# The end of the first attention in a two-block forward pass: where the weights of the next products wait, and how three groups of heads are summed

## The reference

```python
h = rms_norm(h_res, norm_w)                         # 512 tokens x 1024
z = h @ w_in
for g in range(3):                                  # windows and dilations differ by group
    o_g, m_g, d_g = dilated_window_attention(q, k, v, bias, window, dilation)
wts = dens * exp(maxes - max(maxes, axis=0))        # one weight for a group, token and head
o_a = sum(wts * outs, axis=0) / sum(wts, axis=0)
y_a = (o_a * silu(g_a)) @ w_proj_a                  # g_a: 512 columns of z
# the recurrence then begins with its own columns of z
q_b, i_b, zf_fwd, zf_bwd = ...                      # 1024 columns each
lb = cumsum(softmax(lb_fwd), axis=0)                # lower bounds of the decay, one row of 1024
```

## Time and profile before

| | us |
|---|---|
| median of three executions | 4303.97 |
| the profiled execution, its own time | 4302.56 |
| its span, first to last instruction | 4300.8 |
| TensorE busy | 3535.7 |
| mean granted TensorE clock, 1 = 2.4 GHz | 0.895 |
| from the last value product (467) to the first recurrence value product (661.30) | 194 |

### The profile page before, as it was taken

One profiled execution on the slowest core, in us unless ns is written; L12 is line 12 of the kernel. 1 busy time (PEld: TensorE's weight loads), 2 busy tenths in 40 slices (PEclk: granted clock), 3 DMA queues, 4 the chain that ended last, 5 costly groups with the idle time before them and its releaser, 6 DMA issues. The chain is left out here.

```text
span 4300.8 us, 51314 instructions
## 1 busy us (share of the span) xinstructions
PE 3535.7 (82%) x21676; PEld 2057.9 (48%) x21676; DVE 1204.6 (28%) x2331; ACT 639.2 (15%) x1235; POOL 322.4 (7%) x463
## 2 busy tenths in 40 slices
PE   7998678898897877759959999698876899867766
PEld 3767437656552344437833333255766736522222
DVE  2213230232232113867230000033444334320000
ACT  1104100100111011233110000112321012100000
POOL 0000000000000000000011111103534100010000
PEclk9997889988898988879969999899776799889999
DMA  3110122243345120000269999721010201289999
GB/s 127 59 39 1 40 83 88 80 146 115 108 150 205 40 66 9 15 30 1 79 235 396 397 397 394 264 94 30 17 20 13 104 35 67 107 323 401 403 403 358
DMA packets 263928, 638.54 MB, mean 148 GB/s; under 512 B 63876, under 2 KB 114772, under 8 KB 256406
## 3 DMA queue, kind: packets, MB, share of 16 engines
q1 hardware_dynamic: 253654, 612.20, 38.3%
q0 software_dynamic: 10048, 23.07, 2.3%
HBM read 594.18 MB, written 41.05 MB: 148 GB/s over the span
## 5 line engine op out<-in xcount | busy, mean ns | idle before, releaser
L380 PE MATMUL bank<-weights_l,hT_l 128*128 128x256 f32 (+3 forms) x1552 | 485.0, 475 | 24.0 <-DMA weights_l<-in_w_in 19.6
L380 PEld LDWEIGHTS bank<-weights_l,hT_l 128*128 128x128 f32 (+1 forms) x1552 | 337.1, 221 | 169.4 <-issue 103.1
L376 PE MATMUL bank<-hT_l,weights_l 128*128 128x512 f32 (+1 forms) x928 | 332.3, 520 | 29.2 <-DMA weights_l<-in_w_in 23.8
L1739 PE MATMUL bank<-expert_weights_l,expert_tokensT_l 128*32 128x512 f32 x3072 | 339.9, 599 | 10.9 <-DMA expert_weights_l<-in_moe_w 9.4
L1944 PE MATMUL bank<-expert_weights_l,expert_tokensT_l 128*64 128x512 f32 x1024 | 238.4, 611 | 84.3 <-DMA expert_weights_l<-in_moe_w 83.1
L376 PEld LDWEIGHTS bank<-hT_l,weights_l 128*128 128x128 f32 x928 | 179.5, 194 | 179.7 <-issue 155.5
L1242 PE MATMUL bank<-hT_l,gate_weights_r 128*128 128x512 f32 x384 | 211.7, 703 | 21.1 <-DMA gate_weights_r<-in_w_in 21.1
L1739 PEld LDWEIGHTS bank<-expert_weights_l,expert_tokensT_l 128*32 128x32 f32 x3072 | 107.2, 111 | 229.1 <-issue 222.2
L1613 POOL DMA_INDIRECT expert_rows_l<-normed_rows,row_numbers_l x16 | 15.4, 961 | 2630.0 <-DMA row_numbers_l<-selected_rows 2625.7
L1944 PEld LDWEIGHTS bank<-expert_weights_l,expert_tokensT_l 128*64 128x64 f32 x1024 | 78.5, 139 | 233.6 <-issue 175.9
L1774 PE MATMUL bank<-expert_weights_l,rows 128*32 128x512 f32 x1536 | 167.8, 592 | 0.9 <-ACT rows L1814 0.9
(11 more groups left out here) (495 smaller groups left out, 4777.2 us busy)
## 6 DMA issues: line engine op xcount, KB each, us to landing
expert_weights_l<-in_moe_w SPq DMA_DIRECT2D x192, 2048.0 KB, 25.1
ada_weights_r<-in_ada_w SPq DMA_DIRECT2D x48, 1024.0 KB, 5.0
weights_l<-in_w_in SPq DMA_DIRECT2D x10, 2048.0 KB, 7.7
weights_l<-in_w_in SPq DMA_DIRECT2D x16, 1024.0 KB, 5.3
gate_weights_r<-in_w_in SPq DMA_DIRECT2D x12, 1024.0 KB, 6.1
weights_l<-in_od_w_in SPq DMA_DIRECT2D x7, 1024.0 KB, 5.4
gate<-gate_rows_r SPq DMA_DIRECT2D x24, 256.0 KB, 2.4
weights_l<-in_ev_w_in SPq DMA_DIRECT2D x3, 2048.0 KB, 10.5
```

The costliest lines, as they stand in the source:

```text
L376: ins = pe.matmul(bank[:n, :m], w_sb[:, k, s:s + n], xT[:, k, t:t + m], start=k == 0, stop=k == kt - 1)
L380: ins = pe.matmul(bank[:rows_of_tile(x), :n], x, w_sb[:, k, :n], start=k == 0, stop=k == kt - 1)
L1739: return pe.matmul(bank[q * STRIP:(q + 1) * STRIP, :], xs[:, k, e, g * STRIP:(g + 1) * STRIP], w[:, j, h * HALF:(h + 1) * HALF], start=k = ...
```

## The change

- In `first_attention` the gate's weights are loaded into the idle buffer `ya` as soon as SyncE has issued the last weight load of the value products. `merge_groups` gets that view as `ya` and a semaphore.
- `merge_groups` loads `ones` right behind `pair_rows`. After the turned rows it prefetches both chunks of `w_proj_a` and calls `ahead()`, which loads 256 columns of query weights into two idle tiles of `X`.
- The vector chain of the group weights is issued ahead of the gate products, and the gate products run beside it.
- The twelve products follow the gate. Their emptying now does the sums pair by pair: group 0 writes `oT` directly, group 1 is multiplied and added, group 2 is multiplied, added and multiplied by the gate.
- The store of `ya` isn't waited for before the recurrence; `gated_recurrence` takes the 256 query columns as a third ring slot, and prefetches the next two chunks. VectorE waits for the store only after the value products.

```diff
-        self.slot_free = [0, 0]
+        self.slot_free = [0, 0, 0]
...
+            gate_w = ya[:, :, :].rearrange("p t (a n) -> p (t a) n", n=AW)
             with core.weight_ring(512):
                 early = prefetch(core, KT, I["w_in"], 0, AW)
                 first_norm(core, I, C, X, x_landed, ya, hT)
+                normed = core.filled.n
...
+            nc.sync.wait_ge(core.filled.sem, normed)
+            weight_load(gate_w, I["w_in"], KT, OFF_GA, AW)(nc.sync).then_inc(gate_landed.sem, gate_landed.sixteen())
...
     core.load(pair[:, :, :], I["pair_rows"])
+    core.load(C["ones"][:, :, :], I["ones"].rearrange("d s t -> s d t"))
...
     with core.weight_ring(512):
-        dense(core, hT, KT, SEQ, I["w_in"], OFF_GA, AW,
-              lambda e, ct, t0, n, ps: e.activation(gate[:, ct, t0:t0 + n], ps, ACT.Silu),
-              transposed=True, who=lambda i: "s")
+        early = prefetch(core, AW // P, I["w_proj_a"], 0, D)
+        ahead()
         core.settle(dve)
         dve.tensor_tensor(best[:, :], m[:, 0], m[:, 1], ALU.max).then_inc(step.sem, step.one())
...
+        weighed = step.n
+
+        def fill(pe, ct, bank):
+            for k in range(KT):
+                ins = pe.matmul(bank[:, :], ya[:, k, ct * P:ct * P + P], hT[:, k, :], start=k == 0, stop=k == KT - 1)
+            return ins
+
+        pe.wait_ge(gate_landed.sem, gate_landed.n)
+        products(core, PAIRS, fill, lambda e, ct, bank: e.activation(gate[:, ct, :], bank[:, :], ACT.Silu),
+                 lambda i: "s", ready=True)
+        gated = core.emptied_s.n
+        pe.wait_ge(step.sem, weighed)
...
-        products(core, PAIRS * NG, fill, lambda e, i, bank: e.tensor_tensor(
-            u[:, i // NG, i % NG, :], u[:, i // NG, i % NG, :], bank[:, :], ALU.mult))
-        core.settle(dve)
-        dve.tensor_tensor(oT[:, :, :], u[:, :, 0, :], u[:, :, 1, :], ALU.add).then_inc(step.sem, step.one())
-        dve.wait_ge(step.sem, step.n)
-        dve.tensor_tensor(oT[:, :, :], oT[:, :, :], u[:, :, 2, :], ALU.add).then_inc(step.sem, step.one())
-        dve.wait_ge(step.sem, step.n)
-        dve.tensor_tensor(oT[:, :, :], oT[:, :, :], gate[:, :, :], ALU.mult).then_inc(step.sem, step.one())
+        def take(e, i, bank):
+            c, g = i // NG, i % NG
+            here = u[:, c, g, :]
+            if g == 0:
+                return e.tensor_tensor(oT[:, c, :], here, bank[:, :], ALU.mult)
+            linked(e, core.link_v, e.tensor_tensor(here, here, bank[:, :], ALU.mult))
+            ins = e.tensor_tensor(oT[:, c, :], oT[:, c, :], here, ALU.add)
+            if g < NG - 1:
+                return ins
+            linked(e, core.link_v, ins)
+            e.wait_ge(core.emptied_s.sem, gated)
+            return e.tensor_tensor(oT[:, c, :], oT[:, c, :], gate[:, c, :], ALU.mult)
+
+        products(core, PAIRS * NG, fill, take, ready=True)
+        pe.wait_ge(core.emptied_v.sem, core.emptied_v.n)
         dense(core, oT, AW // P, SEQ, I["w_proj_a"], 0, D,
-              lambda e, ct, t0, n, ps: copy(core, e, ya[:, ct, t0:t0 + n], ps), transposed=True, ready=False)
+              lambda e, ct, t0, n, ps: copy(core, e, ya[:, ct, t0:t0 + n], ps), transposed=True, early=early)
...
         with core.weight_ring(256):
-            early = prefetch(core, KT, I["w_in"], OFF_Q, D)
+            core.ring.append(query_w)
+            early = [(2, query_landed.sem, query_landed.n)]
+            early += prefetch(core, KT, I["w_in"], OFF_Q + 2 * P, D - 2 * P)
...
+            dve.wait_ge(spilled.sem, spilled.n)
             yield True
...
-            core.store(spill, ya[:, :, :].rearrange("p t (a n) -> p (t a) n", n=SEQ))
-        core.load(C["ones"][:, :, :], I["ones"].rearrange("d s t -> s d t"))
+            def ahead():
+
+                weight_load(query_w, I["w_in"], KT, OFF_Q, 2 * P)(sp).then_inc(query_landed.sem, query_landed.sixteen())
...
+            sp.wait_ge(core.emptied_v.sem, core.emptied_v.n)
+            sp.wait_ge(core.emptied_s.sem, core.emptied_s.n)
+            sp.dma_start(spill, ya[:, :, :].rearrange("p t (a n) -> p (t a) n", n=SEQ)) \
+                .then_inc(spilled.sem, spilled.sixteen())
```

More of the change, by code:

```diff
@@ L647, in first_norm, with first_attention @@
         products(core, 2 * NT, fill, take, turns, ready=True)
-def first_attention(core, I, C, X, x_landed, hT, ya, scratch):
+def first_attention(core, I, C, X, x_landed, hT, ya, scratch, ahead):
     nc = core.nc
@@ L664, in first_attention @@
         bias_landed = Signal(nc, "attention_bias_landed")
+        gate_landed = Signal(nc, "attention_gate_weights_landed")
         with core.scope() as sb:
@@ L771, in first_attention @@
                 attention_heads(core, flip, sb2, qkT, v, bias, top, den, u)
-        merge_groups(core, I, C, flip, lasting, hT, top, den, u,
-                     ya[:, :, :].rearrange("p t (a n) -> p (t a) n", n=SEQ))
+        merge_groups(core, I, C, flip, lasting, hT, top, den, u, gate_w, gate_landed, ahead)
 V0 = ((0, 64), (64, 192), (192, 320), (320, 448), (448, 512))
@@ L935, in attention_heads, with merge_groups @@
         eng.wait_ge(max_ready.sem, max_ready.n)
-def merge_groups(core, I, C, flip, sb, hT, top, den, u, ya):
+def merge_groups(core, I, C, flip, sb, hT, top, den, u, ya, gate_landed, ahead):
     nc = core.nc
-    dve, act = nc.vector, nc.scalar
+    pe, dve, act = nc.tensor, nc.vector, nc.scalar
     step = core.step
+    merged = Signal(nc, "attention_groups_merged")
     PAIRS = AH // 2
@@ L1052, with gated_recurrence @@
 HB = 4
-def gated_recurrence(core, I, C, hT, oT, spare):
+def gated_recurrence(core, I, C, hT, oT, spare, query_w, query_landed, spilled):
     nc = core.nc
@@ L1261, in first_block @@
             ya = sb2("attention_out", [P, NT, D])
-            first_attention(core, I, C, X, x_landed, hT, ya, scratch)
-            core.store(spill, ya[:, :, :].rearrange("p t (a n) -> p (t a) n", n=SEQ))
-        core.load(C["ones"][:, :, :], I["ones"].rearrange("d s t -> s d t"))
+            spare = X[:, NT:NX, :].rearrange("p t (a b) -> p (t a) b", b=HB * P)
+            query_w = X[:, NT:NX, :].rearrange("p t (a b) -> p (t a) b", b=2 * P)
+            query_landed, spilled = Signal(nc, "query_weights_landed"), Signal(nc, "attention_branch_stored")
+            def ahead():
+                weight_load(query_w, I["w_in"], KT, OFF_Q, 2 * P)(sp).then_inc(query_landed.sem, query_landed.sixteen())
+            first_attention(core, I, C, X, x_landed, hT, ya, scratch, ahead)
+            sp.wait_ge(core.emptied_v.sem, core.emptied_v.n)
+            sp.wait_ge(core.emptied_s.sem, core.emptied_s.n)
+            sp.dma_start(spill, ya[:, :, :].rearrange("p t (a n) -> p (t a) n", n=SEQ)) \
+                .then_inc(spilled.sem, spilled.sixteen())
         with core.scope() as sb2:
@@ L1268, in first_block @@
                 w, rows = beside("gate_weights", [P, KT, 2 * P]), beside("gate_rows", [P, SEQ])
-                weave(gated_recurrence(core, I, C, hT, oT, X[:, NT:NX, :].rearrange("p t (a b) -> p (t a) b", b=HB * P)),
+                weave(gated_recurrence(core, I, C, hT, oT, spare, query_w, query_landed, spilled),
                       gate_products(other, I, hT, w, rows, gates), modulation(other, I, C, mod_dram))
```

## The result

The changed kernel took 4266.09 us (median of four executions, 4264.24 to 4267.44) against 4300.35 us (median of four) before: ratio 0.9917, 95% interval 0.9902 to 0.9932. The forecast was 4264. The profiled execution's span is 4265.4 us against 4300.8, 35.4 us less.

The account below looks back on a forecast made before the run. TensorE, busy 3535.7 of 4300.8 us, was taken as the bound. Terms 9.0 + 2.1 - 0.9 + 13.9 + 9.9 + 14.2 + 2.1 - 11.9 gave 38.4 us (38.8 with rounding), from 4302.56 to 4264; range 4250 to 4281.

Parts of the forecast that it names:

- Gate weights: Before the gate products: the early load removes 9.0 us of waiting and a cold start of 2.1 us.
- Chain of group weights: VectorE's 13.05 us chain runs beside 27 us of gate products and costs nothing; 13.9 us gained.
- Products and sums: Between gate and projection: twelve small products with pairwise sums take 18.9 us instead of 28.8, VectorE setting the pace.
- Projection: After the pairs: TensorE starts cold as before, 30.1 us to the last emptying, ending at 555.9.
- The seam and what is late next: Projection to queries: 14.2 + 2.1 us gained, 11.9 given back waiting for the lower bounds at six banks and restarting cold.
- the queued case: At the seam: the bounds' reads come behind the whole store, so the products of the values begin at 622.5.
- the free one: At the seam: the bounds' reads run beside the store, so the products of the values begin at 618.2.
- (a): Query banks: the lower bounds don't bind, nothing is given back, gain 50.7 us, time 4252; 8 in 100.
- (b): At the seam: bounds and ring chunks share engines with the store worse, gain about 20 us, 4283; 9 in 100.
- (c): In the pairs: half clock of the small products sets the pace, not VectorE; +4.3 us, 4268; 12 in 100.
- (d): Full products from turned rows to values: TensorE stays at 1.2 GHz, up to 109 us lost, 4359; 3 in 100.
- (e): Early load of gate weights or query columns isn't early; 9 to 14 us less, 4273 to 4278; 3 in 100.

Follow-up runs that it names:

- gate_late: Changed kernel with the gate's weights loaded only behind the turned rows; stretch from pair_rows to the products of the values 172.4 us against 159.5, one execution.
- chain_late: Changed kernel with the vector chain of the group weights behind the gate products again; stretch from pair_rows to the products of the values 174.4 us against 159.5.
- exp_early: Changed kernel with one small Exp behind the gate's last Silu; bounds chain 29.85 us against 31.13, stretch from pair_rows to the products of the values 157.2.
- seam_undone: Changed kernel with store waited for, ones loaded and waited for behind it, no third slot; ratio 0.9921 to the kernel before.
- store_behind: Changed kernel with the attention branch's 2 MB store issued behind the bounds' four loads; stretch from pair_rows to the products of the values 153.8 us against 159.5.
- store_waited: Changed kernel with SyncE waiting for the attention branch's store before the ring chunks; stretch from pair_rows to the products of the values 159.7 us against 159.5.

## Why the prediction was right, point by point

- **Ones beside pair_rows.** Expected 0.9 us later: 471.47 - 468.60 = 2.87 against 1.93, 0.94. Not expected: the turned rows then took 8.2 us where they had taken 7.0, the full clock coming back later.
- **Gate weights.** No pause and no cold start between turned rows and gate: 27.7 us, where the sum has 27.3. gate_late puts the part's worth at 13.0 us against the forecast's 11.1.
- **Chain of group weights.** Ended at 493.99 beside the gate; TensorE waited for nothing. chain_late shows the pause of 13.9 us again, and another 4.1 that the sum held under products and sums.
- **Products and sums.** 19.0 us from the end of the gate to the projection against 18.9. The clock fell at about 511.4 (I had said 512). "VectorE sets the pace by a hair" did not hold to the end: from the third pair on VectorE waits three times for a product, once there and twice in the last pair (the row at 522.41 shows one), and its last multiplication starts at 524.12, as the last product ends (507.28 + 16.80). The sum had that product at 522.3; at half clock TensorE set the end. Those waits of 1.3 us in all were offset, because a multiplication from a bank starts about 0.1 us sooner behind another operation than my gap of 0.03 us allows (0.60 to 0.64 from start to start, not 0.72).
- **Projection.** 557.44 - 526.31 = 31.1 us against 30.1. The cold start was longer: the clock rose 5.6 us into the projection, 3.5 us into it before. Stretches of the changed kernel, columns as in the earlier trace rows, show the clock's fall in the small products and the end of the cold start:

```profile
511.00:512.00 1.00, 1.00 (x3) 0.26 (x3) 0.96 (x2) 0.00 (x0) 0.00 (x0) 0.71 0.00 0
...
531.00:532.00 1.00, 1.00 (x2) 0.42 (x2) 0.00 (x0) 0.00 (x0) 0.00 (x0) 0.55 0.00 0
```

- **The seam and what is late next.** The mechanism and its place were those of the forecast: a wait on an emptying behind the sixth query product, 11.9 us where the sum had 9.8, and a cold start behind it. Three terms were too small. The bounds reached VectorE 21.85 us behind the store's issue against 20.2. The chain took 31.1 us and not 29.8: I carried its length over from the earlier trace rows without asking what ScalarE had done last. Before, an Exp of the group weights came after the gate's Silu and left the right table; the change turned that order round, and the load of 1.28 us fell into the chain. exp_early shows it. And the last two products took 16.7 us against 15.8. Together with 0.5 us at the start of the queries, the seam's net of +4.4 us in the sum (14.2 + 2.1 - 11.9) became +0.4, and seam_undone shows it as nothing.
- **The store ahead of the loads.** I took the queued case over the free one; store_behind and store_waited both bear it out. I wrote that no row of the old trace has a store with reads behind it; none that I had listed has, but the trace has one: loads of 1 MB issued 0.4 us behind stores of 256 KB, as at 814.54. What they say of the free or the queued case stays open:

```profile
814.54 0.34 SPq L1250 DMA_DIRECT2D gate<-gate_rows_r  x1
814.93 8.50 SPq L1417 DMA_DIRECT2D ada_weights_r<-in_ada_w  x2
```

  The free case's end was also 0.2 us off: 4.5 us less than 622.5 is 618.0. The Trainium skill's rule ("DMA: Bandwidth & Descriptors", section "Queues, rings and completion order": descriptors are consumed in ring order) agrees with the 0.3 us that waiting for the store cost.
- **The sum.** 32.1 us in the stretch against 38.8. The 6.7 us that are missing are turned rows and gate 1.5, projection 1.0, seam 4.0, rounding the rest. So the forecast was right in what it removed and in where the new wait stands; most of what it missed is the price of that wait. The time, 4266 against 4264, is nearer than the working deserves, and that is luck: 1.1 us ahead of the stretch and 2.2 behind it came by themselves.
- **The rivals.** (a) and (b) are out: the chain binds, the second chunk was in time (571.77, without a wait), and the gain is 32 us and not 20. (c) shows in chain_late at 4.1 us, the 4.3 of its price, where the small products begin cold; in the changed kernel TensorE at half clock set the end of the pairs, but the projection began only 0.1 us later than in the sum (19.0 against 18.9). (d) didn't happen. (e) didn't happen.

## What to carry to other kernels

Before a pause is removed, find what else must be true at its far end, and when: here six banks filled sooner were emptied no sooner behind the last emptying, and 14 us of removed pause came to nothing until a chain of 31 us on other engines was cut. Loading the bounds earlier may be another way out; it was not run. A prefetch can even cost time, here 3 us in one profile, when it moves TensorE's stop from ahead of its work to a place where the last products start cold behind the chain; give its worth only together with the state of the chain that it races. And when two activations change places, ask which table each leaves behind.

## What the runs showed of the hardware

- Behind idle time, products over 8 rows kept the granted clock at 0.50 for 20.8 us of unbroken work; with 120 rows of zeros added, the same instructions brought it to full after 5 to 6 us (13.3 us in all). Between the two only the number of rows differed, and the added ones held zeros. In the turned rows, products over 128 rows into 8 columns, the clock rose 3.3 us behind their start before and 5.8 in the changed kernel. Behind the full-clock gate products it fell in the products over 8 rows, 2.3 us (gate_late) to 4.1 us (changed kernel) into them, though TensorE was busy all the while.
- The time that a cold start costs is not fixed: for the same 64 instructions of the projection 29.2, 29.5, 30.0 and 30.5 us were seen, and for the turned rows 7.0 to 8.2 us. The last two query products behind the banks took 15.4 us (chain_late) to 16.7. My estimate from these spreads (1.3, 1.2 and 1.3 us) is that the three restarts of the changed kernel's stretch can make some 4 us between two profiles.
- Behind a 2 MB store SyncE's own issues took longer: the two ring chunks 2.84 us against 0.99, with the DMA engines' share at 0.89 from 558 to 561. With the store behind them it was 0.99 again. The store's transfers aren't all of it: in store_waited, where they had ended, the same issues took 1.76 us.
- VectorE started an operation that reads a bank 0.60 to 0.64 us behind the start of the one before it where it had nothing to wait for, though each is shown as 0.68 to 0.69 long; operations that waited on the one before kept 0.72.
- On 128x2048 values VectorE's `RECIPROCAL` took 12.95 us, where a `TENSOR_TENSOR` took 2.29.
